# One core, two-layer trunk: the scan and the output projection without a meeting between them, and four modulation pieces moved from the end of layer 0's scan into its attention

## The reference, cut to what matters

```python
for l in range(DEPTH):
    need_ctx = l < DEPTH - 1
    m_lat = (sc @ w_mod[l] + b_mod[l]).reshape(n_b, N_MOD, 1, D_MODEL)
    ...
    h = half_ffn(h, ...)
    y_lat, y_ctx = token_mixing(ul, uc, ...)
    h = h + ml[5] * rms_norm(y_lat, g[3])
    h = half_ffn(h, ...)

def token_mixing(...):
    a_l, a_c = mla_mixer(...)      # attention, 256 features
    b_l, b_c = nat_mixer(...)      # window attention, 256 features
    c_l, c_c = gdn_mixer(...)      # gated delta rule: a scan over 4 chunks
    d_l, d_c = ssm_mixer(...)      # state space: a scan over 4 chunks
    y_lat = jnp.concatenate([a_l, b_l, c_l, d_l], axis=-1) @ w_out
```

## Time and profile before

| | us |
|---|---|
| median of three runs | 2289.8 |
| the profiled execution's own time | 2282.64 |
| its span | 2280.8 |
| TensorE busy with matmuls | 2105.7 (92%) |
| VectorE busy | 1087.8 (48%) |
| ScalarE busy | 810.0 (36%) |
| GpSimd busy | 224.7 (10%) |
| layer 0: last scaling of the scan ends, projection's first matmul, last copy out begins | 837.2, 848.05, 894.09 |
| layer 1: last scaling of the scan ends, projection's first matmul | 2013.8, 2021.86 |

### The profile page before, as it was taken

The page is one execution under the profiler, slowest core; times in us unless marked ns, Lnnn a source line. Parts: engine busy times, 40 slices in busy tenths (PEclk is TensorE's granted clock), DMA queues, the critical chain, the costliest instruction groups (busy, mean ns, idle before and its releaser), DMA issues.

```text
span 2280.8 us, 31525 instructions
## 1 busy us (share of the span) xinstructions
PE 2105.7 (92%) x13261; PEld 1734.4 (76%) x13261; DVE 1087.8 (48%) x1586; ACT 810.0 (36%) x1288; POOL 224.7 (10%) x324
## 2 busy tenths in 40 slices
PE   5999999899988978999999899999979987868997
PEld 4778888687856766788888688888859765767997
DVE  4323333576284565533334633333475557566555
ACT  3322222354345333421223422122344435244343
POOL 0000000100024341000000200000020024420000
PEclk8999999899999989999999899999988999988998
DMA  9464442423224443333423442432332312334662
GB/s 284 129 192 114 125 122 80 147 74 97 74 75 156 161 130 119 86 87 105 109 79 92 120 111 64 126 97 72 119 117 68 121 39 93 112 109 113 176 168 83
DMA packets 403325, 259.07 MB, mean 114 GB/s; under 512 B 21850, under 2 KB 401904, under 8 KB 403184
## 3 DMA queue, kind: packets, MB, share of 16 engines
q1 hardware_dynamic: 403184, 257.06, 38.6%
HBM read 255.97 MB, written 1.05 MB: 113 GB/s over the span
## 4 chain that ended last, share of the span: by engine, by line
PE 80%; DVE 11%; ACT 3%; issue 2%; SPq 1%; POOL 1%; DMA 0%; POOLq 0%; DVEq 0%; ACTq 0%
PE bank L817 23%; PE bank L819 22%; PE bank L818 22%; PE bank L740 2%; PE bank L1164 1%; DVE uT L2012 1%; PE bank L722 1%; DVE wl L1948 1%; ACT wh L1467 1%; DVE mlaw L2267 1%; DVE uT L2010 1%; DVE small L2295 1%; PE bank L761 1%; PE bank L1302 1%; DVE arena L2274 1%
## 5 line engine op out<-in xcount | busy, mean ns | idle before, releaser
L817 PE MATMUL bank<-uh,wh 128*128 128x512 f32 (+1 forms) x1536 | 563.2, 367 | 35.4 <-DVE ul L2018 15.9
L818 PE MATMUL bank<-ul,wh 128*128 128x512 f32 (+1 forms) x1536 | 559.4, 364 | 0.0
L819 PE MATMUL bank<-uh,wl 128*128 128x512 f32 (+1 forms) x1536 | 558.9, 364 | 0.0
L1948 DVE TENSOR_TENSOR wl<-ring,wh 128x2048 fp32r<-128x2048 f32 (+1 forms) x157 | 317.1, 2020 | 171.6 <-ACT wh L1467 170.8
L1467 ACT ACTIVATE wh<-ring 128x2048 fp32r<-128x2048 f32 (+1 forms) x160 | 271.0, 1694 | 316.2 <-PE bank L819 306.1
L817 PEld LDWEIGHTS bank<-uh,wh 128*128 128x128 f32 x1536 | 294.9, 192 | 85.8 <-issue 30.8
L819 PEld LDWEIGHTS bank<-uh,wl 128*128 128x128 f32 x1536 | 294.7, 192 | 44.8
L818 PEld LDWEIGHTS bank<-ul,wh 128*128 128x128 f32 x1536 | 295.0, 192 | 43.5
L817 PE MATMUL bank<-hh,wh 128*128 128x512 f32 (+1 forms) x704 | 255.5, 363 | 1.5 <-DVE wl L1948 1.5
L818 PE MATMUL bank<-hl,wh 128*128 128x512 f32 (+1 forms) x704 | 255.2, 362 | 0.0
L819 PE MATMUL bank<-hh,wl 128*128 128x512 f32 (+1 forms) x704 | 255.2, 362 | 0.0
(11 more groups left out here) (307 smaller groups left out, 2709.8 us busy)
## 6 DMA issues: line engine op xcount, KB each, us to landing
ring<-in_ffn_w_dram SPq DMA_DIRECT2D x176, 512.0 KB, 5.1
ring<-in_w_mod_dram SPq DMA_DIRECT2D x136, 512.0 KB, 4.5
ring<-in_ffn_w_dram SPq DMA_DIRECT2D x64, 384.0 KB, 3.5
ring<-in_ffn_w_dram SPq DMA_DIRECT2D x64, 320.0 KB, 4.1
ring<-in_w_in_dram SPq DMA_DIRECT2D x40, 512.0 KB, 4.7
ring<-in_w_out_dram SPq DMA_DIRECT2D x16, 512.0 KB, 4.5
arena<-in_w_mod_dram SPq DMA_DIRECT2D x8, 512.0 KB, 9.0
ring<-in_w_in_dram SPq DMA_DIRECT2D x4, 544.0 KB, 4.4
```

The lines of the kernel that those rows point to most:

```text
L817: pe.matmul(bank, w_hi, x_hi, start=first, stop=False)
L818: pe.matmul(bank, w_hi, x_lo, start=False, stop=False)
L819: return pe.matmul(bank, w_lo, x_hi, start=False, stop=last)
L1948: TT(low[:, b, 0:floats], at, high[:, b, 0:floats].bitcast(F32), ALU.subtract).then_inc(wl_ready, 1)
```

## The change

- In layer 0 the four modulation pieces behind the scan go into attention: 15 pieces over 16 pairs, one in each but pair 0.
- The meeting between scan and output projection goes.
- The first output weight piece gets buffers of its own (`wh_out`, `wl_out`), rounded by ScalarE in the scan's last step and split by VectorE there. ScalarE also rounds blocks 0 to 3 of `uT` there, and GpSimd makes all four low parts.
- TensorE computes the part k = 0 to 3 of output blocks m = 0 and 1 before it turns the scans' results, and the rest behind them.
- In step 3 VectorE takes the state-space result straight from PSUM (`last_y`) and gates it, which ScalarE and GpSimd did. The scaling of the first two tiles (layer 0) goes from VectorE to GpSimd (`first_scale`).
- ScalarE copies each turned bank straight to `uh`, VectorE makes its low part straight from the bank; `uT` isn't written.
- In each step VectorE adds the part of `o_tm` that comes from the state before it waits for the part within the chunk.
- Some semaphores are merged, with the same waits.

```diff
-        MIX_PIECES = ((11, 8, 4, 4), (5, 4, 4, 0))
+        MIX_PIECES = ((15, 8, 4, 0), (5, 4, 4, 0))
...
+        wl_out, wh_out = rounded("wl_out", 16384, 1, 2048), rounded("wh_out", 18432, 1, 2048)
...
+        def early_out(l):
+            return len(mix_mods(l)[3]) == 0
+        def out_low(eng, l, k):
+            eng.wait_ge(ul_pool if k < 4 else ul_ready, split_before(l, "out") // 2 + k % 4 + 1)
```

On TensorE:

```diff
             def scan_out(l):
-                mod_work(*mix_mods(l)[3], banks=(0, 2))
-                pe.wait_ge(mod_copied, mix_mods(l)[3][1])
+                mods = mix_mods(l)[3]
+                mod_work(mods.start, mods.stop, banks=(0, 2))
+                pe.wait_ge(mod_copied, mods.stop)
+                pe.wait_ge(sem("y_taken"), outputs_before(l, NT))
+                if early_out(l):
+                    out_blocks(l, (0, 1), range(0, 4))
                 pe.wait_ge(sem("scan_normed"), outputs_before(l, NT) // 2)
...
+            def out_proj(l):
+                if early_out(l):
+                    out_blocks(l, (0, 1), range(4, KC))
+                    out_blocks(l, range(2, KC), range(KC))
...
                 scan(l)
                 scan_out(l)
-                meet()
-                out_proj(l, post_halves(l, 1))
+                out_proj(l)
```

On ScalarE, in the scan's step n and behind the steps:

```diff
                     mod_row_out(g, ps[4])
+                    if n == NT - 1:
+                        if len(halves(l, True)) == 2:
+                            finish_roots(l, 0)
+                        else:
+                            load_sqrt()
+                        if early_out(l):
+                            act.wait_ge(sem("sc_ready"), k + 1)
+                            round_out(l)
                     mod_column_out(g, ps[4])
-                    if not state_only(l, n):
+                    if not state_only(l, n) and n < NT - 1:
...
+                for m in range(4):
+                    A(uh[:, m, t0:T], uT[:, m, t0:T], ACT.Copy).then_inc(uh_ready, 1)
...
+                finish_roots(l, 1)
...
                 for b in range(4):
                     act.wait_ge(sem("scan_feature_major"), 4 * l + b + 1)
-                    at = (195, 195, 193, 194)[b]
-                    A(uT[:, 4 + b, t0:T], ps[b][:, t0:T], ACT.Copy, scale=prm[:, l, at:at + 1])
+                    A(uh[:, 4 + b, t0:T], ps[b][:, t0:T], ACT.Copy, scale=prm[:, l, NORM_AT[b]:NORM_AT[b] + 1]
+                      ).then_inc(uh_ready, 1)
```

On VectorE, in the scan's step n and behind the steps:

```diff
-                    elif len(halves(l, True)) == 2:
-                        finish_scale(l, 0)
+                    else:
+                        if len(halves(l, True)) == 2:
+                            finish_inverses(l, 0).then_inc(sem("first_inverses"), 1)
+                        if early_out(l):
+                            split_out(l)
+                        last_y(l, ts)
 
                     if outputs:
+                        add_state(n, ts, [gate(2, d, 0) for d in range(2)])
                         dve.wait_ge(sem("og_ready"), f + 1)
-                        add_out(n, ts, [gate(2, d, 0) for d in range(2)])
+                        add_out(n, ts)
...
                 finish_sums(l, 1)
-                finish_scale(l, 1)
+                finish_scale(l)
+                for b in range(4):
+                    dve.wait_ge(uh_ready, split_before(l, "out") + 4 + b + 1)
+                    STT(ul[:, 4 + b, t0:T], ps[b][:, t0:T], prm[:, l, NORM_AT[b]:NORM_AT[b] + 1],
+                        uh[:, 4 + b, t0:T].bitcast(F32), ALU.mult, ALU.subtract).then_inc(ul_ready, 1)
...
+            def last_y(l, ts):
+                f = outputs_before(l, NT - 1)
+                dve.wait_ge(sem("ys_ready"), NT * (l + 1))
+                dve.wait_ge(sem("y_added"), 2 * f)
+                for d in range(2):
+                    last = TT(heads(y_state[:, d, :]), heads(ps[7][:, d * 256:(d + 1) * 256]),
+                              wide(gates[:, 2, ts[d], d * 8 + 4:d * 8 + 8], 64), ALU.mult)
+                for d in range(2):
+                    y = y_tm[:, ts[d], :]
+                    last = TT(y, y, ps[6][:, d * 256:(d + 1) * 256], ALU.add)
+                last.then_inc(sem("y_taken"), 1)
+                dve.wait_ge(sem("y_taken"), f + 1)
+                for d in range(2):
+                    y = y_tm[:, ts[d], :]
+                    last = TT(y, y, y_state[:, d, :], ALU.add)
+                last.then_inc(sem("y_added"), 2)
+                dve.wait_ge(sem("y_added"), 2 * f + 2)
+                y = y_tm[:, 2:4, :]
+                TT(y, y, zgS[:, 2:4, 0:256], ALU.mult).then_inc(sem("y_gated"), 1)
```

On GpSimd, behind the scan's steps:

```diff
+                if len(halves(l, True)) == 2:
+                    first_scale(l)
                 pool.wait_ge(sem("ys_ready"), NT * (l + 1))
-                add_y(l, NT - 1)
-                gate_y(1)
+                t0 = first_out(l)
+                for m in range(4):
+                    pool.wait_ge(uh_ready, split_before(l, "out") + m + 1)
+                    G.tensor_tensor(ul[:, m, t0:T], uT[:, m, t0:T], uh[:, m, t0:T].bitcast(F32), ALU.subtract
+                                    ).then_inc(ul_pool, 1)
```

More of the change, by code:

```diff
@@ L512, in mix_mods @@
             assert a + b + c + d == MOD_PLAN["mix", l]
-            return range(g, g + a), range(g + a, g + a + b), range(g + a + b, g + a + b + c), (g + a + b + c, g + a + b + c + d)
+            return tuple(range(g + sum(MIX_PIECES[l][:i]), g + sum(MIX_PIECES[l][:i + 1])) for i in range(4))
         def att_pairs(l):
@@ L1366, in out_proj @@
                     pe.wait_ge(y_copied, y_before(l, 1) + m - 1 + Y_CREDIT)
-                    for k in range(KC):
+                    high, low = (wh_out[:, 0], wl_out[:, 0]) if j == 0 else (wh[:, split % 2], wl[:, split % 2])
+                    for k in ks:
                         if m == 0:
-                            wait_low(pe, l, "out", k)
+                            out_low(pe, l, k)
                         ws = slice(k * 256 + b * P, k * 256 + (b + 1) * P)
[L1371 to L1374, removed]
+                        last = split_product(ps[Y_BANKS[b]][:, t0:T], (high[:, ws], low[:, ws]),
+                                             (uh[:, k, t0:T], ul[:, k, t0:T]), k == 0, k == KC - 1)
+                    if KC - 1 in ks:
+                        last.then_inc(pieces_done if b else y_mixed, 1)
+            def out_proj(l):
[3 more added lines that the diff above has]
+                else:
+                    out_blocks(l, range(KC), range(KC))
             def store():
@@ L2500, in finish_scale, with add_state, add_out @@
                    ).then_inc(sem("scan_normed"), 1)
-            def add_out(n, ts, egc):
-                for d in range(2):
-                    if n:
-                        last = TT(heads(tmp_o[:, d, :]), heads(ps[1][:, d * 256:d * 256 + 256]), wide(egc[d], 64),
-                                  ALU.mult)
+            def add_state(n, ts, egc):
+                for d in range(2 if n else 0):
+                    last = TT(heads(tmp_o[:, d, :]), heads(ps[1][:, d * 256:d * 256 + 256]), wide(egc[d], 64),
+                              ALU.mult)
                 if n:
                     link(last)
+                if n % 2:
+                    for d in range(2):
+                        last = TT(o_tm[:, ts[d], :], o_tm[:, ts[d], :], tmp_o[:, d, :], ALU.add)
+                    link(last)
+            def add_out(n, ts):
                 for d in range(2):
@@ L2750, in _ @@
                 scan(l)
-                meet()
-                low_rest(l, "out", HALF * post_halves(l, 1)[0], uT, uh, ul)
                 split_first(PIECES["up0", l, 1][0], 2048)
```

127 lines of the change are left out of this document (69 added, 58 removed).

## The result

The changed kernel takes 2268.9 us in the median of seven runs (2266.2 to 2276.4), the kernel before beside it 2288.8; the ratio is 0.9921 [0.9907, 0.9936] (the brackets are a 95% interval), some 18 us (the two medians differ by 20). The same two kernels once more gave 2268.0 and 0.9907 [0.9893, 0.9921], some 21. It is faster, inside the range of 2267 to 2284 near its lower end, and gains 4 to 7 us more than the 13.6 that I had summed. The band that I had called the likely one, a gain of 11.4 to 18, ends where the measured gain begins.

The account below looks back on a forecast made before the run. TensorE was taken to bound the kernel, so gains lay where it stood still. Layer 0's 11.5, layer 1's 7.0 and the state part's 0.6, less 5.5 in attention, gave 13.6 us: median 2276, range 2267 to 2284.

Parts of the forecast that it names:

- The band that I had called the likely one: Whole kernel: a gain of 11.4 to 18 us, given a chance of 0.59.
- its walk: Scan-to-projection junctions, instruction by instruction on the profiled clock: net gains of 11.5 us in layer 0, 7.0 in layer 1.
- VectorE's tail: VectorE's work from scan end to turning: turning starts 2.7 us later in layer 0, 1.75 in layer 1.
- Turning to first matmul: TensorE, turning to first late projection matmul: 10.7 becomes 3.65 us in layer 0, 7.9 becomes 1.94 in layer 1.
- Early matmuls and clock: TensorE, 24 matmuls before turning and less slow clock: gains 5.4 and 1.8 us in layer 0, 2.9 and 1.1 in layer 1.
- the first rival: Junction: low parts late or clock low, so early matmuls end behind the scaling; gain 6 to 8, time 2283, chance 0.18.
- State part first: Scan steps: adding the state's part first fills 0.3 us of VectorE waiting at each of two steps; 0.6 gained.
- The pieces: Layer 0's attention: four moved modulation pieces cost 8.7 us, less 3.2 as long waits shrink, so 5.5.
- The table load: ScalarE, ahead of the weight rounding: taken as 1.28 us; with a 2.7 budget the gain would be 2.8 smaller.
- The ring: Layer 0's attention: slow 1 MB loads at 130 GB/s would make it 16 us slower, time 2306, chance 0.02.
- The rival by which attention absorbs the pieces and the tail doesn't grow: Attention and junction: pieces cost 2 us, tail 2 to 3 shorter; gain 19 to 20, time 2270, chance 0.1.

## Why the prediction was right, and where its sizes were off

**The sign and the places** are those of the prediction. In layer 0 its walk gave 11.5, the profile has 12.9; in layer 1 7.0 and 7.9.

- **VectorE's tail**, forecast 2.7 and 1.75 later, measured 1.8 and 0.9. Its walk had the split end 2.5 us after it began (3.1 measured), the two additions take 3.1 (2.71), the gate 1.9 (1.65), and the state part with its two additions 2.0, in turns with a fourth low part. They took 1.5 (0.74 and 0.76): GpSimd was done by 835.1 and no turn was left. The turns themselves are right: the two additions took 0.76 a pair alone and 2.71 beside GpSimd, the gate 0.69 alone (layer 1) and 1.65 beside it.
- **Turning to first matmul**: forecast 3.65 and 1.94, measured 3.2 and 1.9. The step held. What I left small in it, the meeting, is 1.9 and 1.2 by the run that put it back.
- **Early matmuls and clock**, layer 0: 5.4 + 1.8 = 7.2 forecast, 46.0 - 38.8 = 7.2 measured. The two 7.2 agree by some luck: in this profile the clock was back at 2.4 GHz when the late part began, so it gave 2.3 and not 1.8, and TensorE paused 0.4 ahead of the second weight piece's matmuls. In the profile taken again it was back later, and the part is 39.5. The margin of 0.2 us that fed the first rival was 3.7. I had costed m = 1 at 0.42 a matmul, the low clock, and they ran 0.227 apart, 2.3 us in all. And GpSimd had its last low part done at 831.5 on the clock of before, not 833.6, so m = 1 began at 832.5 and not 834.8. The turning came 0.9 earlier than forecast, which took that much off. In layer 1 2.9 + 1.1 - 1.3 = 2.7 forecast, 2.8 measured; the run with the second piece early took the stall away and gained 1.2.
- **State part first**: 0.6 forecast. In layer 0 three scan steps took 48.5 and 48.2 at the same clock, so 0.3 at most.
- **The pieces**: 5.5 forecast. The work was 6.1 and the clock gave 2 back, so A to B grew by 4.0 to 4.2. The mechanism held in part. The waits at the turned row (L732 after) are

```profile
PE bank L732 <- ACT mod_row L1462: 8.5, 15, 1.4
```

15 that sum to 8.5, where 11 summed to 8.7. What they have beyond 0.50 each was 3.2 and is 1.0, so 2.2 shrank away, not all 3.2: 8.7 - 2.2 = 6.5 by that step, against the 6.1 of work measured. What the step did not foresee is the clock.
- **The table load** stood at 1.28 us, and the rounding of the first piece behind it ended at 826.8, which is 823.2 on the clock of before (B is 3.6 later), where the walk had 823.3. By the Trainium skill's budget (ScalarE: Activation LUTs, Rules for kernel authors), about 2.7 us a switch, it would have ended 1.4 later. The trace doesn't agree: ScalarE's instruction ahead of the load ends at 823.17, the load runs from 823.18, and the next begins at 824.48; the forecast without the budget was the nearer.
- **What the sum had no term for** is the stretch behind the last junction: 239.2 became 236.4, and 237.2 the second time, with the same matmuls (x1708 in both rows above). The rows show the clock at 0.93 and 0.95. The four profiles without an early part in layer 1 have 238.6 to 239.2 and the ten with it 236.4 to 238.0, so it goes with the early part. The clock is not all of it: with the squares on ScalarE the stretch is 238.0 at 0.93. What else makes it shorter is not shown.

The sum of what was mis-sized: 1.4 + 0.9 in the junctions, 0.9 for A to B (4.9 net forecast, 4.0 measured), 2.0 to 2.8 behind, 5 to 6 us, against the 4 to 7 that the timed 18 to 21 has over 13.6. None of the rivals took place. The ring fed attention at 182 GB/s. The rival by which attention absorbs the pieces and the tail doesn't grow has the time (2270) and the gain (19 to 20) nearest to the measured ones, but both grew, so it is right by number only. The forecast was right by its mechanism, with its gains put a little too low and its costs a little too high.

## What to carry to other kernels

Where two stages meet, cost the chain that must be refilled behind the meeting, not the meeting: here 1.9 of 7.5 us was the barrier, as measured by putting it back. Work that moves ahead of a junction pays if its engine stood waiting there for another one (TensorE's early matmuls), and costs where that engine ends last (the split, 1.8 us of VectorE's tail). Count also what had to be moved to make room: here the four pieces cost 6.1 us in attention, more than the 3.6 that the early part of layer 0 won. Moving elementwise work from VectorE to GpSimd to relieve it can lose (0.8 us here), because the two slow each other down. And set stretches between the same events beside each other before believing a difference of two whole profiles, for the clock elsewhere can hide a third of it.

## What the runs showed of the hardware

- Two-input operations on SBUF of VectorE and GpSimd slow each other by the other's size: a pair of 128x256 additions took 0.76 us alone, 1.76 beside 128x256 low parts on GpSimd, 2.71 beside 128x512 ones. A 128x2048 subtraction took 2.28 or 2.29 us on VectorE alone, 3.12 beside GpSimd's, and 4.57 on GpSimd. GpSimd's four low parts took 5.30 to 7.22 with what VectorE did beside them. The Trainium skill (SBUF — State Buffer, Summary: rules for kernel authors) has the second of two such instructions wait until the first is done. The 2.71 agree with that: they are 0.76 and two waits of about 1 us, and a 128x512 operation on GpSimd takes 1.28.
- The same work gets a different amount of low clock in each execution: 58 to 89 us between the two junctions in the four profiles of before and after, and the stretch was 976.1 to 982.4 us long with it.
- Matmuls whose result nobody wants can shorten what stands behind them: eight ahead of the turning brought it from 3.41 to 1.97 us. By themselves (12 and 40 of them) they took 1.2 us off the two handovers, less than the times can tell, and in layer 1 TensorE then waited longer for the second weight piece, 1.89 us instead of 0.83.
